# Expert blocks of 64 rows in two TensorE column tiles, gate and up weights laid out by eight neighbouring rows, and the S5 Toeplitz blocks in 32-column tiles

## What is computed

```python
# s5_mixer: xi is a linear recurrence over time of (u @ B); y = C_re xr - C_im xi
_, _, xr, xi = lax.associative_scan(_complex_affine_combine, (a_r, a_i, bu_r, bu_i), axis=1)
# hier_moe: 4 groups of 8 experts; the best group, then its best 2 experts for each token
gsel = jnp.argmax(xn @ w_rg + b_rg, axis=-1)
top_p, top_i = lax.top_k(softmax(logits of the 8 experts of gsel), 2)
expert = gsel[:, None] * 8 + top_i
def expert_block(xb, e):
    h = jax.nn.silu(xb @ w_gate[e]) * (xb @ w_up[e])     # 1024 -> 512
    return h @ w_down[e]                                 # 512 -> 1024
# each token's two results are weighted by its gates and added to h
```

## Time and profile before

| | us |
|---|---|
| time, median of 3 runs (lowest to highest) | 2454.18 (2447.6 to 2457.45) |
| time of the profiled execution | 2454.5 |
| its span, first to last instruction | 2452.7 |
| around the span | 1.8 |
| S5 with the cross-attention weights | about 770 to 882 |
| first to last product of the experts | 1586.4 to 2395.0 |
| last add landed, `finish` begins | about 2408 |

### The profile page before, as it was taken

One profiled execution on the slowest core, in us unless ns is written; L12 is line 12 of the kernel. 1 busy time (PEld: TensorE's weight loads), 2 busy tenths in 40 slices (PEclk: granted clock), 3 DMA queues, 4 the chain that ended last, 5 costly groups with the idle time before them and its releaser, 6 DMA issues. The chain is left out here.

```text
span 2452.7 us, 34881 instructions
## 1 busy us (share of the span) xinstructions
PE 2269.7 (93%) x11993; PEld 1292.3 (53%) x11994; DVE 1406.5 (57%) x2047; ACT 986.8 (40%) x1418; POOL 366.0 (15%) x275
## 2 busy tenths in 40 slices
PE   7999999999979998999999999399999999999990
PEld 3565565655668974555555555144544545445440
DVE  7566555665569753333333332777557677777753
ACT  5432433323221342222222221256446576666653
POOL 0021121210220000000000000012222223222222
PEclk9999999999989998999999999599999999999995
DMA  7001001002051152111111100579677899998957
GB/s 249 39 27 61 1 27 61 1 27 46 9 214 35 44 188 96 36 69 44 61 69 51 45 35 35 181 260 313 212 241 271 292 316 320 333 307 300 318 179 289
DMA packets 155062, 349.50 MB, mean 142 GB/s; under 512 B 28496, under 2 KB 39120, under 8 KB 154704
## 3 DMA queue, kind: packets, MB, share of 16 engines
q1 hardware_dynamic: 140128, 310.32, 34.8%
q0 software_dynamic: 13680, 33.58, 5.8%
q10 hardware_dynamic: 1152, 4.19, 0.4%
HBM read 303.48 MB, written 60.82 MB: 149 GB/s over the span
## 5 line engine op out<-in xcount | busy, mean ns | idle before, releaser
L111 PE MATMUL bankA<-main_room,hnT 128*128 128x512 f16 (+1 forms) x1536 | 302.2, 355 | 4.1 <-DVE main_room L639 4.1
L111 PE MATMUL bankE<-wg,xT 128*128 128x512 f16 x1128 | 254.3, 382 | 5.9 <-DVE xT L2542 5.6
L111 PE MATMUL bankE<-wd,hT 128*128 128x512 f16 x1128 | 251.2, 379 | 2.6 <-DVE hT L2547 2.6
L111 PE MATMUL bankE<-wu,xT 128*128 128x512 f16 x1128 | 251.1, 379 | 0.0
L111 PEld LDWEIGHTS bankA<-main_room,hnT 128*128 128x128 f16 x1536 | 150.8, 99 | 146.9 <-issue 9.0
L111 PEld LDWEIGHTS bankE<-wg,xT 128*128 128x128 f16 x1128 | 110.9, 99 | 141.9 <-issue 11.9
L111 PE MATMUL bankA<-hnT,main_room 128*128 128x512 f16 x768 | 172.5, 387 | 8.9 <-issue 6.8
L111 PEld LDWEIGHTS bankE<-wd,hT 128*128 128x128 f16 x1128 | 109.9, 98 | 126.3 <-issue 3.5
L111 PEld LDWEIGHTS bankE<-wu,xT 128*128 128x128 f16 x1128 | 110.4, 98 | 122.7
L111 PE MATMUL bankC<-w_out_s,catT 128*128 128x512 f16 x768 | 171.3, 384 | 2.5 <-DVE w_probs L1914 2.5
L2519 DVE SCALAR_TENSOR_TENSOR wg<-w_rows,wg 128x2048 f16<-128x2048 f32 x64 | 143.7, 2287 | 49.9 <-ACT wg L2294 49.9
(11 more groups left out here) (389 smaller groups left out, 3276.7 us busy)
## 6 DMA issues: line engine op xcount, KB each, us to landing
w_rows<-in_w_gate SPq DMA_DIRECT2D x64, 1024.0 KB, 8.5
w_rows<-in_w_up SPq DMA_DIRECT2D x64, 1024.0 KB, 8.1
w_rows<-in_w_down SPq DMA_DIRECT2D x64, 1024.0 KB, 10.3
cat_t<-scratch_cat SPq DMA_DIRECT2D x16, 512.0 KB, 4.8
main_room<-in_x SPq DMA_DIRECT2D x16, 512.0 KB, 5.5
scratch_ybuf<-main_room SPq DMA_DIRECT2D x16, 512.0 KB, 2.6
out<-hf SPq DMA_DIRECT2D x16, 512.0 KB, 11.0
x_room<-in_x SPq DMA_DIRECT2D x3, 2048.0 KB, 10.8
```

What stands on the lines that cost most here:

```text
L111: ins = pe.matmul(o, a[x][k], b[y][k], start=start and k == 0 and j == 0, stop=stop and k == n - 1 and j == 2)
```

## The change

- **Blocks of 64 rows.** A block's tokens are the 64 columns of the weights operand (`xT`, `hT`), and two matmuls stand side by side in the array: half 0 writes partitions 0 to 63 and half 1 partitions 64 to 127 of the same bank. For gate and up the halves are columns 0 to 255 and 256 to 511 of both matrices (a moving operand of 256 gate and 256 up columns), for down they are the two halves of the 1024 outputs. So a block has 48 matmuls of 512 columns for gate and up and 24 for down; ACT, DVE and POOL handle operands of half the size on 128 partitions.
- **Order.** Two blocks are in flight (`p` is 0 or 1): own halves of `xr`, `xT`, `sg`, `hT`, `y`, own banks. x is turned two blocks ahead, gathered four ahead, and the down product is of block b-2. All four pieces of gate and up are split in one turn, the down pieces in the next.
- **Layout.** Gate and up weights are loaded as `(p k)`: partition p gets rows 8p to 8p+7, a piece being four of them, 8 KB in one run. To match, DVE writes the normed tokens for the router and experts dealt (column k*128+q is channel 8q+k), reading its operands in steps of eight elements. The router's weights lie in the same way. A gathered or added row is now half a token, 2 KB.
- **Lists.** They have 98 columns in place of 64; the gate list needs seven instructions less on DVE. `in_block` lies in slot 1 of the gate and up weights, so ACT splits expert 1 only after the gate list is made.
- **S5.** Each Toeplitz block is made of four matmuls with 32 columns of weights at four places of the array, and each again for the odd step: 8 matmuls as before, of 32 columns each.

```diff
@@ s5_mixer, PE
-                    for s in range(SBL):
-                        a = (SBL - 1 - s) * S5C
-                        ins = pe.matmul(bank[3][:, gg * P:(gg + 1) * P], BZ[:, gg, a:a + LK], CZ[:, q % 2, gg, a:a + LK],
-                                        start=(s == 0), stop=(s == SBL - 1))
+                    for late in range(2):
+                        b = (SBL - 1 - late) * S5C
+                        for j in range(SBL // 2):
+                            a = (SBL - 1 - 2 * j - late) * S5C
+                            r = slice(2 * j * S5C, 2 * (j + 1) * S5C)
+                            ins = pe.matmul(bank[3][r, gg * P:(gg + 1) * P], BZ[:, gg, b:b + 2 * S5C], CZ[:, q % 2, gg, a:a + LK],
+                                            start=(late == 0), stop=(late == 1), skip_group_check=True)
@@ cross_and_router, DVE
-                dve.scalar_tensor_tensor(XN[c % NXR], H[c % NHR], rs[:, 1, c:c + 1], gf[:, :], ALU.mult, ALU.mult).then_inc(xns, 1)
+                by_row, dealt = "t (q k) -> t k q", "t (k q) -> t k q"
+                dve.scalar_tensor_tensor(XN[c % NXR].rearrange(dealt, k=KT), H[c % NHR].rearrange(by_row, k=KT), rs[:, 1, c:c + 1],
+                                         gf[:, :].rearrange(by_row, k=KT), ALU.mult, ALU.mult).then_inc(xns, 1)
@@ experts, SP
-                rows = dram[name][0].rearrange("e (k p) f -> e p k f", p=P)
+                rows = dram[name][0].rearrange("e (p k) f -> e p k f" if p in GU else "e (k p) f -> e p k f", p=P)
@@ experts, POOL
             def gather(b):
-                if b:
-                    pool.wait_ge(xt, 2 * b)
...
+                if b >= 2:
+                    pool.wait_ge(xt, b - 1)
...
             def add(b):
                 if b:
                     pool.wait_ge(y_st, b * 16)
-                pool.wait_ge(y_t, b * 2 + 2)
...
+                pool.wait_ge(y_t, b + 1)
+                pool.indirect_dma_start(to_rows, bass.IndirectOffsetOnAxis(ap=rows[:, b:b + 1], axis=0), y[b % 2], None,
+                                        bounds_check=2 * T - 1, oob_is_err=False, compute_op=ALU.add).then_inc(y_st, 16)
@@ experts, ACT
+            def step(b, p):
+                silu(b, p)
+                take_h(b - 1, 1 - p)
+                take_x(b + 2, p)
+                following(act, b, gate_up_split(b))
+                take_y(b - 2, p)
+                following(act, b - 1, down_split(b - 1))
@@ experts, DVE
+            def step(b, p):
+                product(b, p)
+                h_rest(b - 1, 1 - p)
+                x_rest(b + 2, p)
+                following(dve, b, gate_up_rest)
+                following(dve, b - 1, down_rest)
@@ experts, PE
+            def in_halves(o, tokens, rows, ks, n):
+                for k in ks:
+                    for j, (x, z) in enumerate(((0, 0), (0, 1), (1, 0))):
+                        for half in range(2):
+                            ins = pe.matmul(o(half), tokens(x, k), rows(z, k, half), start=k == 0 and j == 0, stop=k == n - 1 and j == 2, skip_group_check=True)
+                return ins
...
+            def step(b, p):
+                by_slot(b, gate_up(b, p))
+                turn_h(b - 1, 1 - p)
+                turn_x(b + 2, p)
+                by_slot(b - 2, down(b - 2, p))
```

More of the change, by code:

```diff
@@ L2175, in place, with among_first @@
         def place(p, slot, part):
-            _, w, k, a = pieces[p]
-            return w[:, slot, part, k:k + a, :]
+            _, g, k, a = pieces[p]
+            return wd[:, slot, part, k:k + a, :] if g is None else wgu[:, slot, part, k:k + a, g, :]
+        def among_first(b, n):
+            return isinstance(b, int) and b < n
         def following(eng, b, split):
@@ L2245, in _ @@
[L2245 to L2246 removed]
+                pool.wait_ge(y_t, b + 1)
+                pool.indirect_dma_start(to_rows, bass.IndirectOffsetOnAxis(ap=rows[:, b:b + 1], axis=0), y[b % 2], None,
+                                        bounds_check=2 * T - 1, oob_is_err=False, compute_op=ALU.add).then_inc(y_st, 16)
+            for b in range(4):
+                gather(b)
             pool.wait_ge(planned, 1)
             used = turns_used(pool)
[L2250 to L2253 removed]
@@ L2266, in _ @@
-            pool.wait_ge(end_st, 16)
-            pool.wait_ge(x_ld, used * 16 + 48)
+            for r in range(MAX_TURNS + 3):
+                if r <= MIN_TURNS:
+                    for b in (2 * r, 2 * r + 1):
+                        gather(b + 4)
+                        if b >= 2:
+                            add(b - 2)
+                elif r <= MAX_TURNS + 1:
+                    with pool.If(used + 1 > r):
+                        for b in (2 * r, 2 * r + 1):
+                            if b + 4 < NBT:
+                                gather(b + 4)
+                    with pool.If(used + 3 > r):
+                        add(2 * r - 2)
+                        add(2 * r - 1)
+                else:
+                    with pool.If(used + 3 > r):
+                        add(2 * r - 2)
+                        add(2 * r - 1)
@@ L2323, in take_h @@
-            def take_h(b):
-                act.wait_ge(ht, b + 1)
-                act.activation(hT[:, 0, :, :], bank[4][:, :].rearrange("p (k n) -> p k n", k=FT), ACT.Copy, scale=H_SCALE).then_inc(h_hi, 1)
-            def take_y(b, taken=y_t):
-                act.wait_ge(y_st, b * 16)
-                for j in range(2):
-                    act.wait_ge(yd, b * 2 + j + 1)
-                    act.activation(y[:, j * 512:(j + 1) * 512], bank[5 + j][:, :], ACT.Copy, scale=1.0 / (W_SCALE * H_SCALE)).then_inc(taken, 1)
+                    act.wait_ge(yd, b)
@@ L2640, in products_of @@
                     pe.wait_ge(lo_gu, u * 4 + 2)
-                    pe.wait_ge(sil, b)
-                    products(pe, bank[2][:, :], tokens, rows(wg)).then_inc(gd, 1)
-                    if between:
-                        between()
+                    in_halves(o, tokens, rows_of, range(0, KT // 2), KT)
                     pe.wait_ge(lo_gu, u * 4 + 4)
-                    pe.wait_ge(hr, b)
-                    products(pe, bank[3][:, :], tokens, rows(wu)).then_inc(ud, 1)
+                    in_halves(o, tokens, rows_of, range(KT // 2, KT), KT).then_inc(gu, 1)
@@ L2653, in products_of @@
                     pe.wait_ge(h_hi, b + 1)
                     pe.wait_ge(h_lo, b + 1)
-                    if more:
-                        pe.wait_ge(y_t, b * 2)
-                    for j in range(2):
-                        products(pe, bank[5 + j][:, :], [[hT[:, h, n, :] for n in range(FT)] for h in range(2)],
-                                 [[wd[:, slot, h, n, j * 512:(j + 1) * 512] for n in range(FT)] for h in range(2)]).then_inc(yd, 1)
-                return products_of
-            def step(b):
-                by_slot(b, gate_up(b, lambda: turn_h(b - 1)))
-                turn_x(b + 1)
-                by_slot(b - 1, down(b - 1))
+                    if not among_first(b, 2):
+                        pe.wait_ge(y_t, b - 1)
@@ L2680, in _, with last @@
+            def last(n):
+                turn_h(n - 1, 1)
+                by_slot(n - 2, down(n - 2, 0))
+                by_slot(n - 1, down(n - 1, 1))
             steps(pe, first, step, last)
```

352 lines of the change are left out of this document (181 added, 171 removed).

## The result

The changed kernel takes **2390.88 us** (median of 4 runs, 2388.35 to 2396.29). The kernel before, run beside it and earlier, has 2451.73 (4 runs, 2447.60 to 2457.45). The ratio is 0.975, with a 95% interval of 0.973 to 0.977: 61 us faster. The forecast was 2370 in a range of 2334 to 2440. The time lies in the range and in the forecast's own case, 21 us above the point.

What follows compares the result with a forecast made beforehand. PE was taken to bound the experts. From the profiled 2454.5 us, S5 -12, start -0.8, experts -72.5 (691.5 against 764), chunks +1 and end -1 made -85: 2370 us, range 2334 to 2440.

Steps and rivals of the forecast that it cites:

- the forecast's own case: Experts' pace of 8.75 to 9.3 us a block, time 2357 to 2401 us; chance 0.42.
- Pairs side by side, 8.62 us a block: Experts on PE: two matmuls overlap at 0.216 us a pair; with transposes and tile changes a block takes 8.62 us.
- The 17 experts with two blocks go at 18 us: Experts with two blocks: ACT's work with four plan readings makes 18 us an expert, 306 us for 17.
- 8.9: Pace taken for the experts, us a block, bounds 8.6 and 10.9; 77.7 blocks make 691.5 us.
- 16.7 of 17.2 us for DVE: Expert with two blocks: DVE needs 16.7 us for splits and block operations, and PE gives it 17.2.
- Runs of 8 KB cost the same or less: Weight loads by DMA: 8 KB runs in place of 2 KB save between none and a tenth; none taken.
- The additions just under PE, 8.5 us a block: Adds of result rows, each waiting for the last one's landing: 8.5 us a block at a DMA share of 0.85.
- The rival that it sets the pace (10.9): Chain of adds bounds the experts if half rows land no sooner: period 10.9 us, time 2525 us; chance 0.08.
- S5, -12 us: S5 passes: 2.5 us off for three passes and 5.3 for the last, 12 us in all, bounds 5 and 21.
- Chunks +1: Dealt writing of normalised tokens: only the last chunk is on the path, 1 us more, bounds 0 and 8.
- End -1: Last block ends shorter, with two small down products and no empty wait: 1 us less.
- Start: Start of the experts: first product moves from 1607 to 1613, 77.7 blocks left at 1627.6; -0.8 us in the sum.

Runs made afterwards that it cites:

- 8: Kernel 5 with an expert's rows written over the result's rows, no longer added to them: 2356.73 us, ratio 0.961 to the kernel before.
- 3: Changed kernel with gate, up and router weights laid out as before (2 KB runs) and normalised rows written undealt: 2377.04 us, ratio 0.969.
- 11: Changed kernel with each gate and up weight piece loaded in four transfers, 2 KB packets in the new layout: 2379.20 us, ratio 0.971.
- 9: Changed kernel, 8 KB runs kept, with TensorE counting the loop's turn in a register instead of loading it: 2392.11 us, ratio 0.977.
- 5: Kernel 3 with TensorE counting the loop's turn in a register instead of loading it from the plan: 2366.74 us, ratio 0.966.
- 2: Changed kernel with the down product issued as all matmuls of one half, then all of the other: 2497.05 us, ratio 1.019.
- 4: Changed kernel with the loop of the experts unrolled by two, half as many turns: 2623.91 us, ratio 1.070.

## Why the prediction was right, and where it was not

- **Pairs side by side, 8.62 us a block:** right. Pairs take 0.216; with the transposes' 0.81 between the products' starts and ends (0.65 by themselves, the rest changes of tile shape) a block takes 8.70.
- **"The 17 experts with two blocks go at 18 us":** wrong. This is the step that put 8.9 in the sum, by ACT's 15.4 us and four readings of the plan. With the bookkeeping shortened and the additions left out (8) the blocks go at 8.70 apart from up to 0.4 at the turns, with the same splits on VectorE and ScalarE, and from 1624 to 2290 us ACT is busy 463 of 666 us and DVE 505. 16.7 of 17.2 us for DVE was tight, and it held.
- **That the time fell in the forecast's own case is in part luck.** The pace of 9.15 lies within its 8.75 to 9.3, but neither of the two causes of that pace stands in the sum. The pairs and S5 were forecast with their mechanism, the 8.9 was not.
- **The pace that came, 9.15,** has two causes that the sum did not have: **the sequencer's turn**, 25 us, and **late rows**, 9 to 10 us. The first was to be read in the trace of before, where the sequencer's rows stand and the down product that hides them, which was to halve. I asked of each engine whether it keeps up, and not of the one that leads whether it can still be fed.
- **"Runs of 8 KB cost the same or less" (taken as none):** the sign was wrong for the kernel. The engines' own time did fall: q1's share is 36.0% of the span in 3 and 34.8% in the changed kernel. Yet the kernel loses 12 to 14 us, and 11 and 3 show that it is the length of the packets; rows come late at a few blocks.
- **The additions just under PE, 8.5 us a block:** right in kind. Landings are 7.8 us on average in the changed kernel. Additions start 9.0 us apart, PE's pace and not 8.5. POOL waits 249 us for its own landings, which the forecast had as a sign of the chain as the bound if it were most of the time; it is a third of the stretch, and the chain does not set the pace. Without the additions (8) the late blocks are gone. The rival that it sets the pace (10.9) fell.
- **S5, -12 us:** measured -11.0 (1.2, 2.3 and 2.3 in three passes, 5.2 in the last), with PE's wait for L1437 in the pass (2.76 us at 800.21) as the walk had it. **Chunks +1:** 0.8, the longer wait of the last chunk. **End -1:** from PE's last product to the end 56.9 us, before 57.7. **Start:** the fourth gate and up product came 2.4 us later after the router than I had it.

## What to carry to other kernels

When a change halves the time of the instructions on the leading engine, read what its sequencer does between two groups (loads, branches, checks, loop ends) and set it against the lead, which here was some 20 matmuls and shrinks in time with them: some 0.7 us to spare became 0.8 us of stall. Test it by adding one load to both kernels: 1.5 us in one and 17 in the other tells more than any rival's price. A stall taken away shows the next one, so take packet length, and what stands in line behind a transfer that must land, together with it: the same edit gave 10 us with 2 KB packets and nothing with 8 KB.

## What the runs showed of the hardware that was not expected

- Longer packets spare the DMA engines time and cost others theirs. Gate and up packets of 8 KB take 309 ns in the median, four of 2 KB 4 x 84 = 336. With 8 KB the longest landing of an addition was 11.7 us (12.8 in 9), with 2 KB 10.6 (10.7 in 5), while the medians are alike (8.1 and 8.0). These are single profiles, and that the longest landings are what makes the rows late is a reading of them. From issue to landing in the changed kernel, then in the ninth, then in the fifth (us min/median/max, 1624 to 2290 us):

```profile
DMA to landing us min/median/max: 4.3/8.1/11.7
```

```profile
DMA to landing us min/median/max: 4.3/7.9/12.8
```

```profile
DMA to landing us min/median/max: 4.6/7.8/10.7
```

- The two column tiles take work independently: a matmul for the free tile started ahead of three that stood before it in the program and were still to run on the other (2). So the order in which the halves are written matters less than I thought: 106 us, where no pairing in the down product would be 76 x 2.6 = 198.
- A loop whose body doubled stood still for up to 21 us in a turn that should take 35, by the packet counts for the fetch of instructions (4). The counters of the instruction queues show it at once: 236 and 181 packets against 74 and 37.
- After waits of 3.12 and 1.04 us TensorE's granted clock was 0.50 from 1979 to 1984 us (9), so that late row cost its 4.2 us of waits and 2.5 more in the down product. Behind the stalls at the turns the next product took its usual 5.37 us.
